# Cross attention in two halves of heads, input loaded in column halves, output root by reciprocal and square root

## The chip, the cores and the metric

The kernel runs on one core of a Trainium2 chip. The metric is the device time of one execution in microseconds; the median of three timed runs is compared. The core has TensorE (PE in the rows; PEld is its weight load), VectorE (DVE), ScalarE (ACT), GpSimd (POOL) and SyncE (SP), which run their own instruction streams and wait for one another by semaphores.

## The reference, cut to what matters

Activations are x, 256 x 1024 in fp32. Two layers of a first block (three branches: spatial gating, attention, gated linear attention) are followed by one layer of a second block: three mixers, then a cross attention, then a feed-forward and an output norm. The change touches the start of the first layer, the cross attention and the output norm.

```python
def rmsnorm(x, w):
    y = xf * lax.rsqrt(jnp.mean(xf * xf, axis=-1, keepdims=True) + EPS)
    return (y * w)

def memory_cross_attention(h, mem_n, w_q, w_kv, w_o):          # 4 heads of 256, 256 memory rows
    q = (h @ w_q).reshape(b, s, XA_HEADS, XA_HEAD_DIM)
    kk, vv = jnp.split(mem_n @ w_kv, 2, axis=-1)
    ...
    logits = jnp.einsum('bshd,bmhd->bhsm', q, kk) * XA_HEAD_DIM ** -0.5
    p = jax.nn.softmax(logits, axis=-1)
    o = jnp.einsum('bhsm,bmhd->bshd', p, vv).reshape(b, s, XA_HEADS * XA_HEAD_DIM)
    return o @ w_o

x = x + memory_cross_attention(rmsnorm(x, norm_xa_w), rmsnorm(mem, norm_mem_w), w_xq, w_xkv, w_xo)
h = rmsnorm(x, norm_ffn_w)
x = x + jnp.square(jax.nn.relu(h @ w_ff1)) @ w_ff2
return rmsnorm(x, norm_out_w)
```

## The kernel before

Everything stays in SBUF; only the weights stream. x is kept transposed (xT, 8 pieces of 128 columns by 256 rows; two pieces are one group g). A weight product is made from split operands: each operand is a high half (rounded to fp32r by ACT) and a low half (what is left, by DVE), and `split_mm` (L466 to L468) issues three products for one. Weights come in **chunks** of up to 128 x 1024 numbers: SP issues the DMA of chunk c into one of six places of `ring` (L2979), as soon as what used that place is done (`release`); ACT's `weights_hi` makes the high half into one of four places of `ring_hi` (L2343), for which the chunk four before must be used; DVE's `weights_lo` makes the low half (L1341); PE takes the chunk (`take_chunk`). A slot of weight columns is four chunks.

The order of each engine's work is written out by hand. In DVE's and ACT's programs of the second block, `lo_until(n)` and `hi_until(n)` mean: make low or high halves until n chunks of that block are made, then go on with what is written next. Semaphore waits between the engines hold the order together. `open_bank` gives out the eight PSUM banks in turn; a bank is opened when its last use has been freed by the reader (`free`). `hold` keeps the banks of a slot while it accumulates; `copied` waits until a bank has been read out.

**Start.** SP loads the two row halves of x (L2960), then the chunks. POOL issues the DMA of `positions` (L2837), sets `ones` (L2839), the identity and 16 constants (L2845). PE runs seven products of `ones` with itself into an unused bank (L630), then turns the norm's gains (L635) and x (L642), four groups, one bank each. DVE copies each group to xT (L1365); ACT splits from xT (L2326), DVE makes the low half (L1369); chunks 0 to 5 are split between the groups. Slot 0 (`p1(0)`, 416 columns) uses chunks 0 to 3, slot 1 chunks 4 to 7, slot 2 chunks 8 to 11. The squares of x (L2331) are added by DVE (L1376 to L1378), summed over the partitions by PE (L480) behind chunk 4, and `rms` turns the sum into rx (L1385), by shifts and three Newton steps. ACT scales slot 0 by rx on the way out (L2361) and then makes the squares on which the next norm hangs; that norm's root, its scaling and then the low half of chunk 10 follow on DVE.

**Cross attention.** In chunks of the second block: 56 to 59 are the first half of w_xq, 60 to 63 the second, 64 to 67 the last quarter of w_xkv (values of heads 2 and 3; the other keys and values are made earlier), 68 to 75 w_xo. PE's order: xq 0, xq 1, scores of all heads (L1281), the values, turns of the weights (L845), output products (L1294), out projection (wxo). DVE takes maxima and subtracts them (L2242, L2243), ACT takes exponentials of one row half, all heads (L2787), DVE sums and divides (L2248 to L2250), ACT copies the turned weights (L2794) and makes high halves of the outputs (L2355), DVE low halves (L1397).

**Tail.** The last product is made for row half 0 and 1, columns in halves. DVE adds the product to x (L2293), ACT sums the squares (L2823), DVE adds the two sums, scales, and takes the root by `rsqrt` (11 instructions, L1326 to L1331), ACT and DVE scale one column half each, and ACT and SP store it (L2827, L2982).

## Time and profile before

| | |
|---|---|
| timed runs | 1052.29 us median (1050.08, 1052.29, 1054.33) |
| profiled execution | 1050.27 us, span 1048.5 us |
| PE busy | 1013.1 us, 97% of the span |
| DVE busy | 750.2 us, 72% |
| ACT busy | 569.4 us, 54% |
| POOL busy | 73.4 us, 7% |
| DMA | 160.56 MB, 153 GB/s on average |
| TensorE clock granted, mean | 0.992 of 2.4 GHz |

The span is the time from the first to the last instruction; the rest of the profiled execution's time lies around it. Busy times overlap between engines. In the rows below a start and a duration are in us from the span's start; what stands in brackets is how long the engine had been idle before the row's first instruction, and what released it.

### The profile page before, as it was taken

The numbers are of one execution on the slowest core, as the hardware profiler recorded it, in microseconds if no ns is written. First come the engines' busy times: TensorE is split into PE (matmuls) and PEld (weight loads), VectorE is DVE, ScalarE is ACT, GpSimd is POOL, SyncE is SP. The second block draws the span as 40 slices with busy tenths as digits, with TensorE's granted clock in tenths as the row PEclk, the third lists the DMA queues.
The fourth block names the chain that finished last, engine by engine and source line by source line (L and its number), as shares of the span: only waits on it lengthen the run. The fifth ranks groups of instructions, "written<-read, shape, count | busy, mean of one in ns | idle before, by whom it ended". The sixth has DMA issues, their size and how long they took to land.

```text
span 1048.5 us, 21688 instructions
## 1 busy us (share of the span) xinstructions
PE 1013.1 (97%) x9123; PEld 929.9 (89%) x9123; DVE 750.2 (72%) x1200; ACT 569.4 (54%) x833; POOL 73.4 (7%) x177
## 2 busy tenths in 40 slices
PE   7999999999999999999999999889999999999996
PEld 6878999999977999999998998778899799998885
DVE  6879677788877966688789868755786566555445
ACT  5775576444765667453568563134354456675332
POOL 8700000020000000011240000000000000000000
PEclk9999999999999999999999999999999999999998
DMA  9645554575665544548787340011364255665551
GB/s 320 181 135 165 140 156 110 158 252 172 197 175 143 150 136 138 142 134 239 181 216 180 107 152 24 23 35 51 121 201 141 84 183 181 176 182 193 188 190 70
DMA packets 73296, 160.56 MB, mean 153 GB/s; under 512 B 6917, under 2 KB 16320, under 8 KB 73200
## 3 DMA queue, kind: packets, MB, share of 16 engines
q1 hardware_dynamic: 70048, 150.59, 47.0%
q0 software_dynamic: 2832, 8.06, 3.9%
q8 instruction: 72, 1.18, 0.5%
q10 hardware_dynamic: 320, 0.53, 0.1%
q14 instruction: 24, 0.20, 0.1%
HBM read 158.11 MB, written 1.05 MB: 152 GB/s over the span
## 4 chain that ended last, share of the span: by engine, by line
PE 88%; DVE 6%; ACT 3%; issue 2%; DMA 1%; SPq 0%; ACTq 0%; DVEq 0%
PE psum L466 24%; PE psum L468 23%; PE psum L467 23%; PE psum L856 2%; PE psum L1008 2%; DMA ring<-in_w_in 1%; DVE ring_lo L1341 1%; PE psum L845 1%; PE psum L697 1%; PE psum L675 1%; PE psum L1294 1%; PE psum L1281 1%; DVE arena L1501 1%; PE psum L689 1%; PE psum L679 1%
## 5 line engine op out<-in xcount | busy, mean ns | idle before, releaser
L1341 DVE TENSOR_TENSOR ring_lo<-ring,ring_hi 128x1024 fp32r<-128x1024 f32 (+4 forms) x292 | 343.6, 1194 | 185.5 <-ACT ring_hi L2343 183.6
L2343 ACT ACTIVATE ring_hi<-ring 128x1024 fp32r<-128x1024 f32 (+4 forms) x292 | 298.9, 1033 | 280.7 <-PE psum L468 258.0
L466 PE MATMUL psum<-hT,ring_hi 128*128 128x256 f32 x904 | 257.5, 285 | 1.5 <-issue 1.5
L467 PE MATMUL psum<-hT,ring_hi 128*128 128x256 f32 x904 | 254.7, 282 | 0.3 <-issue 0.3
L468 PE MATMUL psum<-hT,ring_lo 128*128 128x256 f32 x904 | 254.9, 282 | 0.0
L466 PEld LDWEIGHTS psum<-hT,ring_hi 128*128 128x128 f32 x904 | 171.6, 190 | 3.9 <-issue 3.4
L467 PEld LDWEIGHTS psum<-hT,ring_hi 128*128 128x128 f32 x904 | 171.6, 190 | 0.5 <-issue 0.5
L468 PEld LDWEIGHTS psum<-hT,ring_lo 128*128 128x128 f32 x904 | 171.7, 190 | 0.0
L466 PE MATMUL psum<-ring_hi,hT 128*128 128x512 f32 (+4 forms) x416 | 156.5, 376 | 4.4 <-DVE ring_lo L1341 4.4
L468 PE MATMUL psum<-ring_hi,hT 128*128 128x512 f32 (+4 forms) x416 | 152.7, 367 | 0.0
L467 PE MATMUL psum<-ring_lo,hT 128*128 128x512 f32 (+4 forms) x416 | 152.3, 366 | 0.0
L466 PE MATMUL psum<-arena_r,ring_hi 128*128 128x256 f32 x384 | 108.9, 284 | 2.2 <-DVE flag L1400 1.5
L467 PE MATMUL psum<-arena_r,ring_hi 128*128 128x256 f32 x384 | 108.2, 282 | 0.0
L468 PE MATMUL psum<-arena_r,ring_lo 128*128 128x256 f32 x384 | 108.2, 282 | 0.0
L466 PEld LDWEIGHTS psum<-ring_hi,hT 128*128 128x128 f32 x416 | 78.6, 189 | 19.0 <-issue 5.8
L468 PEld LDWEIGHTS psum<-ring_hi,hT 128*128 128x128 f32 x416 | 78.5, 189 | 11.2
L467 PEld LDWEIGHTS psum<-ring_lo,hT 128*128 128x128 f32 x416 | 78.6, 189 | 10.8 <-issue 0.5
L466 PEld LDWEIGHTS psum<-arena_r,ring_hi 128*128 128x128 f32 x384 | 72.8, 190 | 3.1 <-DVE flag L1400 1.9
L468 PEld LDWEIGHTS psum<-arena_r,ring_lo 128*128 128x128 f32 x384 | 72.9, 190 | 0.0
L467 PEld LDWEIGHTS psum<-arena_r,ring_hi 128*128 128x128 f32 x384 | 72.8, 190 | 0.0
L2361 ACT ACTIVATE arena<-psum 128x384 f32<-128x384 f32 (+4 forms) x103 | 52.4, 582 | 29.6 <-PE psum L1008 12.5
L466 PE MATMUL psum<-ring_hi,arena_r 128*128 128x512 f32 x128 | 50.3, 393 | 0.4 <-DVE ring_lo L1341 0.4
(453 smaller groups left out, 1345.6 us busy)
## 6 DMA issues: line engine op xcount, KB each, us to landing
ring<-in_w_in SPq DMA_DIRECT2D x104, 512.0 KB, 3.6
ring<-in_w_ff SPq DMA_DIRECT2D x64, 512.0 KB, 3.6
ring<-in_w_branch SPq DMA_DIRECT2D x24, 512.0 KB, 3.7
ring<-in_w_out SPq DMA_DIRECT2D x24, 512.0 KB, 3.5
ring<-in_w_in SPq DMA_DIRECT2D x24, 384.0 KB, 3.3
ring<-in_w_xkv SPq DMA_DIRECT2D x16, 512.0 KB, 3.7
ring<-in_w_in SPq DMA_DIRECT2D x8, 528.0 KB, 3.7
ring<-in_w_xq SPq DMA_DIRECT2D x8, 512.0 KB, 3.7
```

The costliest lines, as they stand in the source:

```text
L466: mm(b, lhs[0], rhs[0], start=start, stop=False, **how)
L467: mm(b, lhs[0], rhs[1], start=False, stop=False, **how)
L468: return mm(b, lhs[1], rhs[0], start=False, stop=stop, **how)
L675: m = mm(b[:, 0:384], cT[:, k, t * P:(t + 1) * P], wuq[:, k, h * 384:(h + 1) * 384], start=(k == 0), stop=(k == 1))
L679: filled(mm(b, cT[:, 2, t * P:(t + 1) * P], wukv[:, h * BANK:(h + 1) * BANK], start=True, stop=True), ("ukv", l, t, h))
L689: m = turn_(b[0:MQK, k * P:(k + 1) * P], qk[:, t, 4 * g + k, :], ident[:, :])
L697: m = mm(b[:, h * n:(h + 1) * n], qkT[0:MQK, h0 + h, t * P:(t + 1) * P], qkT[0:MQK, MH + h0 + h, 0:n], start=True, stop=True)
L856: m = mm(banks[d][q, h * n:(h + 1) * n], lhs(d, h, q), rhs(d, h, q), start=True, stop=True)
L1008: m = mm(banks[z][CH * to:CH * to + CH, o:o + CH], rhs[0](c, odd, d, p, slice(CH * row, CH * row + CH)), rhs[1](c, odd, d, p, slice(CH * r ...
L1341: V.tensor_tensor(chunk_view(ring_lo, RAW, c), chunk_view(ring, RAW, c), plain(chunk_view(ring_hi, RING_HI, c)), ALU.subtract).then_inc(ev ...
L2343: AC(chunk_view(ring_hi, RING_HI, c), chunk_view(ring, RAW, c), ACT.Copy).then_inc(ev("whi_ready"), 1)
L2361: af(AC(dst, b, func, scale=scale), free(name))
```

## The change

- Start: x is loaded in two column halves; the second is issued behind chunk 0. POOL issues the DMA of positions behind the 16 constants. ACT runs one small Copy at once. PE's products of ones are twelve, and seven more behind the turns of the first half of x. The turns of the second half come behind chunk 0 of slot 0. ACT and DVE split x from PSUM; the copy to xT comes behind the squares, which ACT now makes from PSUM. Chunk 0 is split in halves, and PE can begin with the first. The sum of squares on PE comes behind chunk 5.
- Cross attention: heads 0 and 1 go through scores, softmax and outputs before heads 2 and 3. The values' chunks are spread over the order, and so is the start of the out projection. The chunk order in the ring follows that.
- Tail: each sum of squares is scaled and added in one instruction; the root is ACT's Sqrt of DVE's reciprocal, with one Newton step for three; an idle Sqrt stands ahead of it. At row half 1, DVE's share of the scaling is done on a product made before.

```diff
-            w_cols(A["w_xq_2"][0], BANK * i, BANK)
-        w_cols(A["w_xkv_2"][0], BANK * 3, BANK)
+        w_cols(A["w_xq_2"][0], 0, BANK)
+        w_cols(A["w_xkv_2"][0], BANK * 3, BANK, part=range(1))
+        w_cols(A["w_xq_2"][0], BANK, BANK)
+        w_cols(A["w_xkv_2"][0], BANK * 3, BANK, part=range(1, CHUNKS))
         for i in range(2):
             w_rows(A["w_xo_2"][0], 4 * P * i)
...
+                    w = take_chunk(first and c == 0)
                     n = w[0].shape[2] // parts
+                    if first and c == 0:
+                        for j in range(2):
+                            if j:
+                                pe.wait_ge(ev("xlo_ready"), x_parts[0])
+                                pe.wait_ge(ev("wlo_ready"), 1)
+                            for t in range(T):
+                                m = split_mm(banks[(*tag, t, 0)][:, 0:n], parts_of(lhs, j, slice(t * P, (t + 1) * P)),
...
+                for _ in range(n):
+                    mm(psum[:, 7, 0:P], ones[:, :], ones[:, :], start=True, stop=True)
+            warmed(12)
...
-            pe.wait_ge(ev("x_in"), 16 * T)
...
+            def input_turns(half):
+                pe.wait_ge(ev(f"x_in{half}"), 16)
+                for g in (2 * half, 2 * half + 1):
...
+            input_turns(0)
+            warmed(7)
...
-                p1(0)
+                p1(0, {} if l else {0: lambda: input_turns(1)})
...
-                p1(1, {0: squares_sum(l)})
+                p1(1, {0 if l else 1: squares_sum(l)})
...
             x_parts[:] = [KD * 3, CHUNKS]
-            for i in range(2):
...
                         for k in range(2):
                             i = 2 * (2 * g + h) + k
...
+                pe.wait_ge(ev("xp_ready"), g + 1)
...
+            def attention_out(g):
...
+                copied(pe, *[("xpT", t, g) for t in range(T)], *[("xv", g, t, 0) for t in range(T)])
...
+                    filled(m, ("xo", h))
+            gemm_T(("xq", 0), xaT)
+            next(values)
+            squares_sum(3)()
+            attention_scores(0)
+            gemm_T(("xq", 1), xaT)
+            attention_turns(0)
+            next(values)
+            attention_scores(1)
+            attention_out(0)
+            next(values)
+            run(values)
+            attention_turns(1)
+            mixed = rows_T_steps(("wxo",), x_oT, KD, lambda k: pe.wait_ge(ev("lo_made"), SPLITS1 * DEPTH + 6 + (k // 2 + 1 if k < 6 else XH)))
+            next(mixed)
+            next(mixed)
+            attention_out(1)
+            run(mixed)
...
+                b = full(dve, ("x0", g))
...
+                dst = xT[:, 2 * g:2 * g + 2, :].rearrange("p a b -> p (a b)")
+                dve.wait_ge(ev("sq_ready"), g + 1)
...
+                lo_next[0] += 1
...
                 else:
-                    residual(l, ("x0",), R_NORM, (0, 1, 1, 0, 2))
-                weights_lo(2)
+                    input_low(0)
+                    first_weights_lo()
+                    input_low(1)
+                    weights_lo(1)
+                    input_low(2)
+                    weights_lo(1)
+                    input_low(3)
+                    weights_lo(1)
+                    weights_lo(1)
+                    for g in range(4):
+                        input_kept(g)
+                    weights_lo(1)
+                if l:
+                    weights_lo(2)
...
-            lo_until(65)
+            lo_until(63)
...
+                v(V.tensor_reduce(smax[:, 2 * t:2 * t + 2], b, X, ALU.max))
+                vf(V.tensor_tensor(x_s[:, t, 2 * g:2 * g + 2, :], b, bc(smax[:, 2 * t:2 * t + 2], 2, S), ALU.subtract), free(n))
+            def attention_parts(g):
+                for t in range(T):
+                    dve.wait_ge(ev("xe_ready"), 2 * g + t + 1)
+                    v(V.tensor_reduce(ssum[:, 2 * t:2 * t + 2], x_s[:, t, 2 * g:2 * g + 2, :], X, ALU.add))
+                v(V.reciprocal(ssum[:, 0:4], ssum[:, 0:4]))
+                x4 = x_s[:, :, 2 * g:2 * g + 2, :]
+                vf(V.tensor_tensor(x4, x4, bc(ssum[:, 0:4].rearrange("p (t h) -> p t h", t=T), 3, S), ALU.mult), "xp_ready")
...
+            lo_until(66)
+            attention_parts(0)
+            lo_until(69)
             attention_maxima(0, 1)
-            attention_maxima(1, 0)
             attention_maxima(1, 1)
-            attention_parts(0)
             attention_parts(1)
-            lo_until(72)
-            for h in range(XH):
-                b = full(dve, ("xo", h)).rearrange("p (a b) -> p a b", a=2)
-                low(("xo", h), b, x_oT[:, 1, 2 * h:2 * h + 2, :], x_oT[:, 0, 2 * h:2 * h + 2, :], 1.0)
+            attention_low(0)
+            lo_until(73)
+            attention_low(1)
...
-                    vf(V.tensor_tensor(final[:, t, 0, :], xn[:, t * D:t * D + BANK], out_g[:, 0:BANK], ALU.mult))
...
-                v(V.tensor_tensor(rin[:, 0:1], ssq[:, 2 * t:2 * t + 1], ssq[:, 2 * t + 1:2 * t + 2], ALU.add))
-                v(V.tensor_scalar(rin[:, 0:1], rin[:, 0:1], 1.0 / D, EPS, ALU.mult, ALU.add))
-                rsqrt(1)
-                v(V.tensor_copy(rx[:, t:t + 1], rout[:, 0:1]), "final_rms")
...
-                    v(V.scalar_tensor_tensor(out=final[:, t, 1, :], in0=xn[:, t * D + BANK:(t + 1) * D], scalar=rx[:, t:t + 1],
-                                             in1=out_g[:, BANK:D], op0=ALU.mult, op1=ALU.mult), "out_ready")
...
+                dst = xn[:, t * D + c0:t * D + c0 + n]
+                b = full(dve, ("f2", t, c0 // BANK))[:, c0 % BANK:c0 % BANK + n]
+                v(V.scalar_tensor_tensor(out=dst, in0=b, scalar=rx_more[:, t:t + 1], in1=dst, op0=ALU.mult, op1=ALU.add), "out_sum")
+                flat = final[:, t, :, :].rearrange("p h n -> p (h n)")
+                vf(V.tensor_tensor(flat[:, c0:c0 + n], dst, out_g[:, c0:c0 + n], ALU.mult))
+            def out_square(i, before):
+                dve.wait_ge(ev("final_ssq"), i + 1)
+                if before is None:
+                    v(V.tensor_scalar(rin[:, i:i + 1], ssq[:, i:i + 1], 1.0 / D, EPS, ALU.mult, ALU.add))
                 else:
-                    vf(V.tensor_scalar(final[:, t, 0, :], final[:, t, 0, :], rx[:, t:t + 1], None, ALU.mult), "out_ready")
+                    v(V.scalar_tensor_tensor(out=rin[:, i:i + 1], in0=ssq[:, i:i + 1], scalar=1.0 / D, in1=rin[:, before:before + 1],
+                                             op0=ALU.mult, op1=ALU.add))
+            def out_root(t, i):
+                r, y, z = rin[:, i:i + 1], rout[:, t:t + 1], rtmp[:, t:t + 1]
+                v(V.reciprocal(z, r), "final_inverse")
+                dve.wait_ge(ev("final_root"), t + 1)
+                v(V.tensor_tensor(z, y, y, ALU.mult))
+                v(V.scalar_tensor_tensor(out=z, in0=z, scalar=-0.5, in1=r, op0=ALU.mult, op1=ALU.mult))
+                v(V.scalar_tensor_tensor(out=rx[:, t:t + 1], in0=z, scalar=1.5, in1=y, op0=ALU.add, op1=ALU.mult), "final_rms")
+                vf(V.tensor_scalar(final[:, t, t, :], final[:, t, t, :], rx[:, t:t + 1], None, ALU.mult), "out_ready")
+            out_piece(0, 0, BANK)
+            out_piece(0, BANK, BANK)
+            out_square(0, None)
+            out_square(1, 0)
+            out_root(0, 1)
+            out_piece(1, 0, BANK)
+            out_square(2, None)
+            out_piece(1, BANK, BANK)
+            out_square(3, 2)
+            out_root(1, 3)
...
+                    if i == 0:
+                        act.wait_ge(ev("xlo_ready"), 2 * g + 2)
+                    src = xT[:, 2 * g:2 * g + 2, :] if i else full(act, ("x0", g)).rearrange("p (a b) -> p a b", a=2)
+                    af(AC(x_sq[:, 2 * g:2 * g + 2, :], src, ACT.Square), "sq_ready")
...
+                b = full(act, ("x0", g))
+                for k in (2 * g, 2 * g + 1):
+                    af(AC(hT[:, 0, k, :], b[:, k % 2 * S:(k % 2 + 1) * S], ACT.Copy, scale=cols[:, R_NORM + k:R_NORM + k + 1]),
...
+                act.wait_ge(ev("raw_full0"), landed(0))
+                for j, name in enumerate(("whi_half", "whi_ready")):
+                    AC(chunk_view(ring_hi, RING_HI, 0)[:, j, :], chunk_view(ring, RAW, 0)[:, j, :], ACT.Copy).then_inc(ev(name), 1)
...
             act.dma_start(rows[R_NORM:R_MIX, :], A["norm_g"].rearrange("l (k p) -> (l k) p", p=P)).then_inc(ev("norm_in"), 16)
+            act.wait_ge(ev("ones_ready"), 1)
...
                 else:
-                    residual_hi(("x0",), R_NORM, 0)
+                    copied(act, "norm_cols")
+                    input_hi(0)
+                    first_weights_hi()
+                    input_hi(1)
                     weights_hi(1)
-                    residual_hi(("x0",), R_NORM, 1)
+                    input_hi(2)
                     weights_hi(1)
-                    residual_hi(("x0",), R_NORM, 2)
-                    weights_hi(1)
-                    residual_hi(("x0",), R_NORM, 3)
-                    weights_hi(1)
-                squares()
-                weights_hi(6)
+                    input_hi(3)
+                    weights_hi(2)
+                squares(l)
+                weights_hi(6 if l else 5)
                 act.wait_ge(ev("rx_ready"), l + 1)
                 p1(0)
...
+            def attention_exp(g):
...
                 act.wait_ge(ev("xs_scale"), 1)
...
+                for t in range(T):
+                    copied(act, ("xs", t, g))
+                    s1 = x_s[:, t, 2 * g:2 * g + 2, :].rearrange("p h n -> p (h n)")
+                    af(AC(s1, s1, ACT.Exp, scale=rx_more[:, t:t + 1]), "xe_ready")
+            def attention_turned(g):
...
+            def attention_high(g):
...
+            hi_until(65)
+            attention_exp(0)
+            hi_until(68)
+            copy_out(("xq", 1, 0), xq_T[:, 4:6, :], BANK, shape=2)
+            copy_out(("xq", 1, 1), xq_T[:, 6:8, :], BANK, shape=2)
+            attention_turned(0)
+            hi_until(69)
+            attention_exp(1)
+            attention_high(0)
+            hi_until(70)
+            memory_v(1)
             hi_until(72)
-            for h in range(XH):
-                high(("xo", h), x_oT[:, 0, 2 * h:2 * h + 2, :], 2)
+            attention_turned(1)
+            hi_until(73)
+            attention_high(1)
...
+            a(AC(rtmp[:, 2:3], rx[:, 0:1], ACT.Sqrt))
...
+                a(AC(at(proj_all, 2048, n), xn[:, t * D + c0:t * D + c0 + n], ACT.Square, accum_out=ssq[:, i:i + 1]), "final_ssq")
...
+                act.wait_ge(ev("final_inverse"), t + 1)
+                a(AC(rout[:, t:t + 1], rtmp[:, t:t + 1], ACT.Sqrt), "final_root")
                 act.wait_ge(ev("final_rms"), t + 1)
                 h = 1 - t
                 a(AC(final[:, t, h, :], final[:, t, h, :], ACT.Copy, scale=rx[:, t:t + 1]), "half_ready")
                 act.dma_start(out[0, t * P:(t + 1) * P, h * BANK:(h + 1) * BANK], final[:, t, h, :]).then_inc(ev("stored"), 16)
+            out_sums(0, 0, 0, BANK)
+            out_sums(1, 0, BANK, BANK)
+            out_root(0)
+            out_sums(2, 1, 0, BANK)
+            out_sums(3, 1, BANK, BANK)
+            out_root(1)
...
-            pool.dma_start(posi[:, :], A["positions"].rearrange("a (t p) -> p (a t)", p=P),
...
+                           allow_slow_non_contiguous=True).then_inc(ev("pos_in"), 16)
             def masks():
...
         @block.sync
         def _(sp_):
-            for t in range(T):
-                sp_.dma_start(xn[:, t * D:(t + 1) * D], A["x"][0, t * P:(t + 1) * P, :]).then_inc(ev("x_in"), 16)
+            def input_half(half):
+                sp_.dma_start(at(xn, 0, T, D)[:, :, half * BANK:(half + 1) * BANK],
+                              A["x"][0].rearrange("(t p) d -> p t d", p=P)[:, :, half * BANK:(half + 1) * BANK]).then_inc(ev(f"x_in{half}"), 16)
+            input_half(0)
             for c, (parts, _, _) in enumerate(chunks):
+                if c == 1:
+                    input_half(1)
```

## Rows read from the trace of the kernel before

**Rows 1.** Page, part 1: busy time, share of the span, instructions.
```profile
PE 1013.1 (97%) x9123; PEld 929.9 (89%) x9123; DVE 750.2 (72%) x1200; ACT 569.4 (54%) x833; POOL 73.4 (7%) x177
```

**Rows 2.** Page, part 4: the chain that ended last, by engine.
```profile
PE 88%; DVE 6%; ACT 3%; issue 2%; DMA 1%; SPq 0%; ACTq 0%; DVEq 0%
```

**Rows 3.** Chain of waits in order of time (start us, us, what), start.
```profile
1.73 6.61 DMA ring<-in_w_in
8.37 0.91 ACT ring_hi L2343
```

**Rows 4.** Timeline from 0 to 34 us (start us, us, engine, line, operation, tiles).
```profile
1.27 1.28 ACT L2326 ACT_TABLE_LOAD   x1 [1.27 <-PEq L3000]
1.33 0.87 POOL L2837 DMA_DIRECT2D posi<-in_positions  x1 [0.81 <-POOLq L3000]
...
2.48 3.16 PE L630 MATMUL psum<-ones 128*128 128x128 f32 x14 [2.48 <-POOL ones L2839]
...
10.47 0.42 PE L466 MATMUL psum<-ring_hi,hT 128*128 128x416 f32 x1 [2.67 <-DVE ring_lo L1341]
...
16.16 0.43 PE L466 MATMUL psum<-ring_hi,hT 128*128 128x416 f32 x1 [0.72 <-DVE ring_lo L1341]
...
20.77 0.26 PE L657 MATMUL psum<-ident,arena 107*128 107x107 f32 x1
```

**Rows 5.** DMA rate, 0 to 20 us in 40 slices of 0.5 us.
```profile
GB/s 0 0 0 8 147 377 369 377 442 390 306 137 107 223 276 369 396 403 406 402 411 401 411 406 397 401 397 410 374 221 268 395 471 373 406 381 426 418 393 424
```

**Rows 6.** Timeline of ACT, then of DVE, 17 to 60 us.
```profile
29.46 1.11 ACT L2361 ACTIVATE proj<-psum,rx 128x416 f32<-128x416 f32 x2 [0.77 <-DVE rx L1385]
...
36.15 1.22 DVE L1341 TENSOR_TENSOR ring_lo<-ring,ring_hi 128x1024 fp32r<-128x1024 f32 x1
```

**Rows 7.** Timeline of PE: the first instruction on chunk 10.
```profile
38.71 0.39 PE L466 MATMUL psum<-ring_hi,hT 128*128 128x512 f32 x1
```

**Rows 8.** PE's waits, 785 to 857 us (total us, times, longest).
```profile
PE psum L466 <- DVE flag L1400: 1.5, 1, 1.5
PE psum L1294 <- ACT arena L2794: 1.1, 1, 1.1
PE psum L1281 <- issue: 0.8, 1, 0.8
```

**Rows 9.** Timeline of PE, windows within 800 to 827 us.
```profile
804.50 1.75 PE L1281 MATMUL psum<-proj,arena 128*128 128x256 f32 x7 [0.84 <-issue]
...
811.29 0.58 PE L466 MATMUL psum<-ring_hi,hT 128*128 128x512 f32 x1
...
822.57 1.91 PE L845 MATMUL psum<-ident,arena 128*128 128x128 f32 x16
```

**Rows 10.** Timeline of DVE and ACT, softmax.
```profile
806.50 0.69 DVE L2242 TENSOR_REDUCE smax<-psum 128x2 f32<-128x512 f32 x1
...
814.66 1.23 DVE L2250 TENSOR_TENSOR arena<-arena,ssum 128x1024 f32<-128x1024 f32 x1
...
809.79 1.15 ACT L2787 ACTIVATE arena<-arena,rx_more 128x1024 f32<-128x1024 f32 x1 [4.57 <-issue]
```

**Rows 11.** Timeline of the tail.
```profile
1041.74 0.19 ACT L2823 ACTIVATION_READ_ACCUMULATOR proj<-xn 128x1 f32 x1
1041.96 0.16 DVE L2300 TENSOR_TENSOR rin<-ssq 128x1 f32<-128x1 f32 x1
...
1044.71 0.72 ACT L2826 ACTIVATE proj<-proj,rx 128x512 f32<-128x512 f32 x1 [2.78 <-DVE rx L2303]
```

**Rows 12.** Groups of ACT's instructions over the span (busy us, mean ns).
```profile
L2683 ACT ACTIVATE rtmp<-na_sum 128x1 f32<-128x1 f32 x4 | 0.8, 202 | 0.1
...
L2468 ACT ACT_TABLE_LOAD x2 | 2.6, 1283 | 0.0
```

**Rows 13.** Stretches (from:to, length, busy by engine, PEclk, DMA share, GB/s).
```profile
664.00:667.00 3.00, 1.22 (x51) 1.02 (x45) 2.78 (x6) 0.18 (x1) 0.00 (x0) 1.00 0.00 0
667.00:672.00 5.00, 4.31 (x144) 3.94 (x144) 3.88 (x14) 1.01 (x3) 0.00 (x0) 0.66 0.01 3
```

159 lines of the change are left out of this document (71 added, 88 removed).

## Prediction

> **What bounds the kernel now.** I read the page first. PE is busy 1013.1 of 1048.5 us [rows 1], and the chain that ended last is 88% PE [rows 2]. The change removes no product of PE, so it can only win where PE stands still, or where the chain leaves PE: at most the other 12%. The diff touches three such places: the start, the cross attention (about 785 to 857 us) and the tail behind the last product. I then read each from the view that shows what ends last there: chain and timeline for the start, PE's waits for the attention, the timeline for the tail. The profiled execution took 1050.27 us, its span 1048.5; the median of the three timed runs is 1052.29, their mean 1052.2 (1050.08 to 1054.33). The sum is made against 1050.27 and then carried to the timed runs.
>
> **The start.** Today the chain begins with the DMA of weight chunk 0, issued at 1.73 and landed 6.61 us later, at 8.34; ACT makes its high half at 8.37 in 0.91 [rows 3], DVE the low half, and the first product runs at 10.47; PE waits 2.67 us for that [rows 4]. Why so late a landing? The DMA rate is about 370 to 440 GB/s from 2.5 us on, then falls to 137 and 107 GB/s in two slices near 6 us and comes back only near 7.5 [rows 5], though chunks are queued. The positions DMA, 4 byte elements on POOL's queue, was issued at 1.33 [rows 4]. I take it to be the cause (the row shows the coincidence, not the cause). The change issues it behind POOL's 16 constants, and orders half of x, chunk 0, other half, chunk 1. In front of chunk 0 then lie 0.5 MB and not 1.0, which at 400 GB/s is 1.3 us less, and no dip: chunk 0 at about 6.0. So the landing stops ending last, and what is next is PE's warm-up.
>
> The positions issue also leaves POOL's path to the memset of ones: 0.87 us earlier, so the warm-up starts at about 1.6 and not 2.48 [rows 4]. It has 12 products for 7, two instructions each. The 14 of today take 3.16 us, 0.226 each; 24 at that rate end at 7.0. A two-instruction product of the attention, 256 wide, takes 0.25 per instruction at full clock (7 in 1.75, the pipeline's end included) [rows 9], so 0.11 at 128 wide; if PE rises to full clock after some 3 us as it must have today, the end is 5.7. I take 6.3. Then the gain columns and 4 transposes (0.12 each by 16 in 1.91 [rows 9]): group 0 of x is in PSUM at 7.0. ACT now splits it straight from PSUM (DVE's copy, 0.7 as other 128x512 pieces [rows 10], leaves the path): two ACT pieces, together about one 0.91 piece [rows 3], to 7.9; DVE's low halves as long, to 8.8; the low half of half a chunk, about half of 1.22 [rows 6], to 9.4. The second 7 warm-up products (14 instructions, 1.5 to 3.1 us, from 7.5) end at 9.0 at full clock, hidden, but at 10.6 at half clock, where they would themselves be the bound. First product: 9.4, against 10.47.
> From there PE needs 24 instructions per 4.61 us (16.16 to 20.77 [rows 4]), so 9.2 for the slot; today it takes 10.3, with the wait of 0.72 before 16.16 among it. The new order puts 8 transposes (1.0) inside the slot, which used to lie in idle time, and they cover the waits for the later splits: ACT and DVE alternate x pieces and chunks at 1.8 to 2.1 us per pair against 2.3 of PE's per chunk. End: 9.4 + 9.2 + 1.0 = 19.6 against 20.77, 1.2 us.
> Will it be kept? The next in line is the norm. ACT's copy of slot 0 waits for rx at 29.46, and the low half of chunk 10, behind that same chain, is done at 36.15 + 1.23 = 37.4 [rows 6]; PE takes it at 38.71 [rows 7]. So 1.3 us at most comes through unless rx is earlier too. rx hangs on chunks 6 and 7, whose landing today is late for DMA rate; they are now issued earlier (when chunk 0 is used) but the positions dip still comes, later. DVE's four copies of x to SBUF (0.7 each) now wait for ACT's squares behind the splits, and behind them is queued the low half of chunk 5, due on PE at 22.8, done at about 22. That fits by 0.7 us. The banks of x are freed by those copies, due at 20.0, done from 18.8. I take **1.2 us**, bounds -0.8 (half clock through both warm-ups: 10.6 + 10.2 = 20.8, and 0.7 for chunk 5) and +2.3 (rx moves too). The early table load is worth nothing: the load already runs at 1.27, ahead of all data [rows 4].
>
> **The cross attention.** PE waits in three places: 0.8 before the scores (for the copies of xq 1), 1.1 before the output products (for ACT's copies of the turned weights), 1.5 before the out projection (for DVE's low halves) [rows 8]. Counted from one instruction's start to the next they are 1.0, 1.1 and 1.7, together 3.8. The new order puts other products behind each: chunk 0 of xv (12 instructions at 0.23 wide pace, 2.8 us, from 48 in 822.57 - 811.29 [rows 9]) and the sum of squares after xq 0; xq 1 (11.5) over the first softmax; two chunks of the out projection (5.7) over the turned weights of half 1. I laid out the order from 791.75, where xq 0 ends: xv chunk 794.6, squares 794.9, scores 0 (half of 6.8: 3.4) 798.3, xq 1 809.8, turns 810.8, xv 813.6, scores 1 817.0, outputs 0 820.4, two xv chunks 826.0, turns 827.0, two chunks 832.7, outputs 1 836.1, rest of the projection 853.3.
> DVE and ACT against it: norm until 797.8, low chunk, two maxima and subtractions (4 x 0.69) to about 802, exponentials of half size (0.65; a whole one is 1.15 [rows 10]), low halves of two chunks, sums and one product of 1.23 [rows 10]: first weights at 807.8, needed at 809.8, 2.0 to spare. Copies of xq 1 and of the turned weights 811.7, needed at 813.6. Second softmax at 821.7, needed at 826.0. The closest is ACT's order at 827: copy of xv, high halves of chunks 70 and 71, and only then the copies of the turned weights, done 830.4; PE wants them at 832.7. The instructions are more (eight smaller pieces for four) but neither engine is full here. DVE's new waits (for exponentials) hold up low halves of chunks 66 and 68, due 3 us or more later. The sum is that all 3.8 goes and five more changes of product kind come, at less than 0.1 each: **3.4 us**, bounds 1.5 (one of the spare times misjudged by 2) and 3.9.
>
> **The tail.** From the end of ACT's last sum (1041.93) DVE runs 14 small instructions, 2.75 us (0.196 each), before ACT's scaling at 1044.71 [rows 11]. The change leaves: fused scale and add, reciprocal, ACT root, three for one Newton step. DVE: 5 x 0.196 = 1.0; ACT: 0.20 for one 128x1 activation [rows 12] and two handovers of 0.1 (1041.74 + 0.19 to 1041.96 is 0.03, rx to ACT 0.1): 1.4. Gain **1.4 us**; bounds 1.1 and 1.6 if no table is loaded on the path. Row 0's root falls away too, but was hidden by PE. The load of the root's table (1.28 [rows 12]) comes with the idle root behind the last high half, where ACT only waits for PE's last products: hidden, and 1.3 on the path if that cover were gone. What is last next: ACT's scaling (0.72), issue and landing, all as before.
> Does Square or Copy after the root load a table back? Rows say that loads (1.28 each) come at few lines only [rows 12], and between them the engine ran both kinds in more than one set: the first load is for a Copy [rows 4] and the Squares of the first norm follow without one.
> The Trainium skill, "ScalarE: Activation LUTs", section "Table sets: the hidden batching unit", speaks against the change: exp and root are in different sets, and cheap functions it names as in every set are relu, copy, identity, abs, not Square. By that page each switch is about 2.66 us with its drain; an estimate with two on the path would be -5.3 + 1.4. The trace has 1.28 for the load.
>
> **Sum.** 1.2 + 3.4 + 1.4 = 6.0 us: 1044.3 for the profiled execution, 1046.2 from the timed runs' mean. The profiled one lies 1.9 below it, so I put the forecast a little under the latter: **1045.8**. With the bounds of the terms the total is 1.8 to 7.8; the runs themselves scatter by 2 either way. 0.5% (5.3 us), about what a measurement of this kernel can tell from no change, is 1047.0: the forecast lies just beyond it.
>
> **Rivals.**
> A: the start gives nothing, since rx and the chunk landings set the pace until 38 us (for it: only 1.3 to spare there [rows 6, 7]). 4.8 us in all: 1047.2. Chance 0.15.
> B: one spare time in the attention is misjudged, most likely at 809.8 (2.0) or 832.7 (2.3), and a wait of 2 comes back; 4.0: 1048.0. Chance 0.09.
> C: Square is not in the root's set. Then ACT loads before the last sums and before the root, 1.28 each; the first of them is hidden when it comes early, the second is on the path, the first partly: tail +0.1 to -1.2 (1.4 less 1.28 or 2.56), total 4.0: 1048.2. This is the page's rule as a mechanism here. Chance 0.06, as the rows show Square under two sets.
> D, slower: the granted clock. It is 1.00 on average from 664 to 667, where PE was busy 1.22 of 3.0 us, and 0.66 on average from 667 to 672 [rows 13], right behind. At half clock (0.50, 1.2 GHz) for 2 x 0.34 of 5 us, 3.4 us, this costs 1.7. The changed start shifts everything behind it, and more such stretches can be caught. It decides from the fourth further one (6.8 against 6.0); with six, 10.2 - 6.0 = 4.2 slower, 1056. Against it: the attention had clock 1 throughout, and the gaps that the change leaves there are smaller. Chance 0.05.
> E: rx and landings move too and a half-clock stretch is lost: 8.5, 1043.3. Chance 0.05.
> Forecast: 0.60. The range that leaves out no more than 0.2: the terms' bounds and the scatter, **1041 to 1050.5**. Faster by over 0.5%: 0.45 of the 0.60, 0.05 of A and 0.05 of E, 0.02 of B and C, so 0.57; slower by over 0.5% 0.03 (part of D); the rest, 0.40, within.
>
> **What would show it.** First product at 9 to 10 us, not 10.5, the DMA dip behind chunk 0's landing, slot 0 over by 19.6, and at 38 us no wait of PE for a low half; PE's waits of the attention gone from their list, with first split of the residual 3.4 us sooner relative to xq 0's end; 1.35 to 1.4 between ACT's last sum and its scaling, and one table load more in the whole trace. It is wrong if PE's start is bound by the warm-up at half clock, if a wait appears at the first x banks or chunk 5, or if the root comes with a load beside it.

## The result, and the profile after

The changed kernel takes 1044.58 us (median of eight runs; 1043.2 to 1049.3) against 1050.35 for the one before (eight runs, 1048.51 to 1054.33); the ratio is 0.9942 with a 95% interval of 0.9925 to 0.9959, or 6.1 us (4.3 to 7.9). The forecast was 1045.8, and 6.0 less by the sum of the terms. Ratios use fast runs alone, which leaves out of all the runs one of the kernel before, at 3225 us. The profiled execution took 1044.02 us, its span 1042.3 (before: 1050.27 and 1048.5), so 6.25 less.

The page's busy times and the chain by engine, answering to [rows 1, 2]:

```profile
PE 1016.2 (97%) x9147; PEld 933.6 (90%) x9147; DVE 747.5 (72%) x1188; ACT 571.0 (55%) x841; POOL 71.9 (7%) x177
...
PE 86%; DVE 6%; ACT 3%; issue 3%; DMA 2%; ACTq 0%; POOL 0%; DVEq 0%; POOLq 0%
```

24 instructions of PE more are the warm-up's. What the page can't tell is where the 6.2 us come from. For that I set the start of every PE instruction of one trace against the same one of the other; the table under the experiments has these differences for all kernels. For this one: 0.9 us ahead at 20 us, 0.6 from 40 us, 0.85 behind from 245 us, 0.55 ahead again at 780 us, 4.6 from 858 us, and 6.2 at the end.

**Start.** The timeline of all engines from 0 to 31 us, after (start us, us, engine, line, operation), against [rows 4, 6, 7], and the DMA rate of the first 20 us in slices of 0.5 us, against [rows 5]:

```profile
1.08 5.00 PE L648 MATMUL psum<-ones 128*128 128x128 f32 x24 [1.08 <-POOL ones L2987]
...
6.17 1.09 PE L664 MATMUL psum<-ident,xn 128*128 128x128 f32 x8
...
6.92 0.84 ACT L2452 ACTIVATE hT<-psum,cols 128x256 fp32r<-128x256 f32 x2 [4.12 <-PE psum L664]
...
7.10 1.73 PE L648 MATMUL psum<-ones 128*128 128x128 f32 x14
7.65 0.99 ACT L2460 ACTIVATE ring_hi<-ring 128x416 fp32r<-128x416 f32 x2
...
9.40 0.43 PE L470 MATMUL psum<-ring_hi,hT 128*128 128x416 f32 x1 [0.58 <-DVE ring_lo L1430]
...
19.89 0.26 PE L682 MATMUL psum<-ident,arena 107*128 107x107 f32 x1
...
25.13 1.06 ACT L2446 ACTIVATE ring_hi<-ring 128x1024 fp32r<-128x1024 f32 x1 [0.72 <-DMA ring<-in_w_in]
...
30.08 1.11 ACT L2478 ACTIVATE proj<-psum,rx 128x416 f32<-128x416 f32 x2 [1.27 <-DVE rx L1445]
```
```profile
GB/s 0 0 0 37 70 107 226 367 389 363 395 403 413 406 390 409 393 388 393 394 400 397 385 406 395 380 406 363 270 156 172 205 254 270 369 422 381 418 424 406
```

The dip to 137 and 107 GB/s near 6 us [rows 5] is gone, and the first product runs at 9.40 for 10.47. (The later dip, to 156 GB/s near 15 us, isn't that of the positions: they had landed at 10.26.) At the end of slot 0 it is 19.89 for 20.77. Then part of it goes: the copy that waits for rx comes at 30.08, not at 29.46 [rows 6], and at 38.02 PE starts on chunk 10 some 0.2 us late.

**Cross attention.** One stretch of PE, 780 to 860 us (length, busy by engine, PEclk, DMA share, GB/s), of the kernel before and then of the changed one:

```profile
780.00:860.00 80.00, 76.55 (x543) 72.04 (x543) 50.81 (x77) 39.22 (x54) 0.00 (x0) 1.00 0.43 137
```
```profile
780.00:860.00 80.00, 80.00 (x578) 76.17 (x577) 53.26 (x82) 43.26 (x61) 0.00 (x0) 1.00 0.47 153
```

PE stood still for 3.45 us of this stretch, the three waits of [rows 8], and now not at all. From before it to behind it the lead grows from 0.55 to 4.62.

**Tail.** Its timeline after, ACT and DVE, against [rows 11]:

```profile
1037.10 0.19 ACT L2961 ACTIVATION_READ_ACCUMULATOR proj<-xn 128x1 f32 x1
1037.32 0.16 DVE L2386 SCALAR_TENSOR_TENSOR rin<-ssq,rin 128x1 f32<-128x1 f32 x1
1037.51 0.16 DVE L2392 RECIPROCAL rtmp<-rin 128x1 f32<-128x1 f32 x1
1037.77 0.20 ACT L2966 ACTIVATE rout<-rtmp 128x1 f32<-128x1 f32 x1 [0.48 <-DVE rtmp L2392]
...
1038.71 0.72 ACT L2969 ACTIVATE proj<-proj,rx 128x512 f32<-128x512 f32 x1 [0.74 <-DVE rx L2396]
```

From the end of the last sum (1037.29) to the scaling are 1.42 us, for 2.78. No table load stands between. The one further load of the whole trace is at 1025.0, while PE is still at work on the last products, so it is hidden.

**Near 240 us** the trace has a wait that the one before has not. PE's waits from 200 to 260 us, after (before: none), and ACT's from 200 to 230 us, of before and of after (total us, times, longest):

```profile
PE psum L470 <- DVE hT L1747: 1.0, 1, 1.0
```
```profile
ACT ring_hi L2343 <- DMA ring<-in_w_branch: 4.1, 2, 2.6
```
```profile
ACT ring_hi L2446 <- DMA ring<-in_w_branch: 5.9, 4, 3.8
```

In both kernels POOL issues the second layer's vectors here (2.3 MB, from 210 us on), beside SP's branch weights. After, these weights land later (the chunk issued near 213 us takes 11.1 us to land, for 8.8), and PE is 1.4 us behind for it.

### The profile page after: what moved, and what is told of

The parts are those of the page before. It is cut to its first block, busy times and chain, and to the rows that moved or that the text cites. A ratio compares the mean times of both kernels' runs of the same rounds, so it can differ in the third digit from the quotient of the medians.

```text
span 1042.3 us, 21750 instructions
## 1 busy us (share of the span) xinstructions
PE 1016.2 (97%) x9147; PEld 933.6 (90%) x9147; DVE 747.5 (72%) x1188; ACT 571.0 (55%) x841; POOL 71.9 (7%) x177
## 4 chain that ended last, share of the span: by engine, by line
PE 86%; DVE 6%; ACT 3%; issue 3%; DMA 2%; ACTq 0%; POOL 0%; DVEq 0%; POOLq 0%
PE psum L470 23%; PE psum L472 23%; PE psum L471 22%; PE psum L881 2%; PE psum L1033 1%; PE psum L870 1%; DVE ring_lo L1387 1%; DMA ring<-in_w_branch 1%; PE psum L722 1%; PE psum L700 1%; DVE arena L1573 1%; PE psum L1307 1%; PE psum L714 1%; PE psum L1324 1%; PE psum L704 1%
## 5 line engine op out<-in xcount | busy, mean ns | idle before, releaser
L2446 ACT ACTIVATE ring_hi<-ring 128x1024 fp32r<-128x1024 f32 (+4 forms) x291 | 297.7, 1034 | 267.9 <-PE psum L472 241.9
L472 PEld LDWEIGHTS psum<-ring_hi,hT 128*128 128x128 f32 x416 | 78.1, 188 | 11.1
L2478 ACT ACTIVATE arena<-psum 128x384 f32<-128x384 f32 (+4 forms) x103 | 52.8, 584 | 28.0 <-PE psum L1033 11.8
```

What stands on the lines that cost most here:

```text
L472: return mm(b, lhs[1], rhs[0], start=False, stop=stop, **how)
L2446: AC(chunk_view(ring_hi, RING_HI, c), chunk_view(ring, RAW, c), ACT.Copy).then_inc(ev("whi_ready"), 1)
L2478: af(AC(dst, b, func, scale=scale), free(name))
```

## The experiments

For each kernel its timed ratio to the kernel before, and where its profiled execution gains against that of before. The gains are differences of PE's start times, in us, worked out from the two traces: at 40 us, what is added around 240 us, in the middle (260 to 780), across the attention (780 to 860), and in the tail (the span's gain less that at the last products). A span is that of one execution: those of only_tail and late_proj are the slowest of their kernel's timed runs, that of warm_short the fastest.

```
kernel           ratio, interval          at 40   at 240   middle  attention  tail   span
after            0.9942 0.9925-0.9959      0.6    -1.4      1.4      4.1      1.6    1042.3
only_start       0.9974 0.9961-0.9988      1.1    -0.1      1.3      0.0      0.0    1046.2
only_attn        0.9948 0.9931-0.9964     -0.3     0.0      0.9      4.1      0.0    1043.9
only_tail        1.0016 1.0001-1.0031     -2.8    -2.7     -1.4      0.0      1.6    1053.9
before_again     (one execution)          -0.7     0.0     -1.5      0.0     -0.1    1050.8
warm_short       0.9956 0.9935-0.9977      0.6    -1.4      1.8      4.1      1.5    1042.0
tail_warm        1.0006 0.9991-1.0022     -0.5    -1.1      1.0      0.0      1.5    1047.6
pos_moved        0.9988 0.9965-1.0011     -0.6     0.0      0.6      0.0     -0.1    1048.5
late_proj        0.9983 0.9958-1.0009      0.3    -3.1     -2.0     -0.5      1.6    1052.2
table_back       0.9965 0.9943-0.9986      0.3    -3.0      1.6      4.1      0.3    1045.3
sqrt_only        1.0015 0.9992-1.0039     -1.0    -1.1     -1.3      0.0     -0.1    1052.0
vectors_later    0.9956 0.9940-0.9972      1.1     0.0      2.1      4.1      1.6    1044.1
vectors1_later   0.9921 0.9899-0.9944      0.9     0.0      1.0      4.1      1.6    1041.0
```

(vectors_later loses another 4.4 between 40 and 200 us.)

### The three parts alone, and the kernel before once more

only_start has the diff's edits of the start alone (the orders of x and positions, the warm-ups, the splits from PSUM, chunk 0 in halves), only_attn those of the attention and its chunk order, only_tail those of the tail. before_again is the kernel before, unchanged.

> The kernel before with the start of the change alone. My theory: the first weight product at 9.4 us (10.47 before), slot 0 over 0.9 us earlier, 0.6 us of it left behind 40 us because the norm's rx is not earlier, and no more than 0.6 us on the whole time beside the scatter of the half-clock stretches. Rival: the start is worth what it gains at slot 0 or more (1 us and above), and what was lost behind 38 us in the changed kernel was chance: then PE is 0.9 us or more ahead from 45 us on.

> The kernel before with the cross attention of the change alone. My theory: PE's waits of 0.8, 1.1 and 1.5 us are gone, and the stretch from the end of xq 0 to the end of the out projection is 4.1 us shorter, nothing else: 4 us on the whole time. Rival: part of the 4.1 us in the changed kernel came from its other position in time; then this run shows 3 us or less in that stretch, or a wait that the changed kernel doesn't have.

> The kernel before with the tail of the change alone. My theory: 1.4 us between ACT's last sum and its scaling for 2.75 to 2.8, so 1.4 us on the whole time. Rival: the rest of what the changed kernel gained behind the last product (1.6 us in all) comes from the tail too, with an earlier second store; then 1.6. A table load on the path would make it 0.1 or a loss.

> The kernel before, one more look. Theory: what differs between 40 and 785 us in the traces (half-clock stretches near 579 and 640 us, issue gaps near 710 us, the branch weights' landing at 222 us) varies from execution to execution of one kernel by 1 to 3 us, and the stretches from 785 to 857 us and behind the last product don't, by more than 0.1. Rival: the middle comes out the same to 0.2 us as in the first trace of this kernel, and then its differences belong to the change.

only_start: 2.7 us in the timed runs (1.3 to 4.1), the first product 1.4 and the end of slot 0 1.2 sooner, and 1.1 kept behind 40 us; another 1.3 comes in the middle, all of it at 710 us (under rivals D and E below). only_attn: 5.5 us in the timed runs (3.8 to 7.3), 4.07 in its place, as in the whole. only_tail: slower by 1.7 us (0.1 to 3.3), though 1.42 us stand between the last sum and the scaling there too. Its loss is elsewhere. Its chain at the start (start us, us, what), to set against [rows 3], and stretches of its start (columns as above):

```profile
1.73 8.02 DMA ring<-in_w_in
```
```profile
8.00:10.00 2.00, 0.53 (x5) 0.29 (x3) 1.43 (x3) 1.00 (x3) 1.64 (x4) 1.00 1.00 373
10.00:12.00 2.00, 0.13 (x1) 0.16 (x1) 1.30 (x2) 2.00 (x4) 2.00 (x4) 0.66 1.06 409
12.00:17.00 5.00, 5.00 (x15) 4.77 (x16) 4.93 (x10) 4.13 (x9) 4.29 (x13) 0.50 1.08 339
```

The start is that of the kernel before, instruction for instruction, and yet chunk 0 lands 1.4 us later (8.02 for 6.61). PE stands still for 3.3 us and then runs at a granted clock of 0.50, the lower level (1.2 GHz), to 17.5 us. So the old start has executions that lose 2.8 us: 1.4 by the late landing (first product at 11.87, for 10.47), 1.4 by the clock behind it. before_again puts a size to the chance in one trace: 0.7 at the start (chunk 0 lands at 8.99) and 1.5 in the middle, for nothing; its attention and its tail agree with those of before within 0.1. The columns of attention and tail can be read to 0.1 us. The sums in those of start and middle can't be read to 1 us, unless one looks where in them the time goes.

### The start: warm-up and positions

warm_short is the changed kernel with the old warm-up:

```diff
-            warmed(12)
+            warmed(7)
...
             input_turns(0)
-            warmed(7)
```

tail_warm is only_tail with seven warm-up products between x's turns and the first layer:

```diff
                 filled(m, ("x0", g))
+            for _ in range(7):
+                mm(psum[:, 7, 0:P], ones[:, :], ones[:, :], start=True, stop=True)
```

pos_moved is the kernel before with the positions' DMA behind the constants:

```diff
-            pool.dma_start(posi[:, :], A["positions"]...)
             g(G.memset(ones[:, :], 1.0), "ones_ready")
...
                 g(G.memset(freq[:, i:i + 1], ...
+            pool.dma_start(posi[:, :], A["positions"]...)
```

> The changed kernel with the warm-up of before: seven products and none behind the turns. Theory A (the added products buy a steady clock): the first weight product comes at about the same time or 0.5 us sooner, but PE idles before it and a half-clock stretch appears in the first 20 us in some or all executions, costing 1.5 to 3.5 us on the median. Rival B: the longer warm-up is itself what ends last at 6 us (24 instructions until 6.1), and shorter is 0.5 to 0.8 us faster.

> The tail alone, and seven more products of ones behind PE's turns of x, where PE idled from 8 to 11.8 us in the run of the tail alone. Theory: the tail alone was slower than its 1.4 us gain allows because the clock fell to half from 10.6 to 17.4 us behind that idle time (4.0 us of idle and 6.8 us at half clock in its trace); the products keep PE busy there, the clock stays at full, and the whole time falls from 1053.8 to below the kernel before, by some 3 to 4 us. Rival: the half clock is chance and not tied to the idle time, or the tail itself costs: then the time stays near 1053 and a half-clock stretch stands in the first 20 us again.

> The kernel before with only the DMA of the positions moved behind POOL's constants. Theory 1, this DMA makes the dip of the DMA rate near 6 us: the slices at 137 and 107 GB/s rise to 350 or more (or the dip goes with it to a later time), chunk 0 lands 0.6 to 1.5 us sooner, and the first product comes 0.3 to 1.2 us sooner, bounded by the warm-up and the copies of x, which come no sooner by more than POOL's 0.87 us. Rival: the dip is from the order of x and weights on the queues; then it stays at 6 us in place and size, the landing of chunk 0 stays within 0.3 us, and so does the first product.

Stretches of warm_short, then of the changed kernel cut alike in vectors1_later (same start):

```profile
5.00:8.00 3.00, 1.06 (x8) 0.82 (x8) 1.32 (x3) 2.28 (x6) 2.48 (x9) 0.97 1.04 387
8.00:12.00 4.00, 3.64 (x12) 3.51 (x13) 2.44 (x5) 1.07 (x2) 3.69 (x6) 0.60 1.05 399
```
```profile
8.00:12.00 4.00, 3.42 (x22) 3.18 (x22) 3.30 (x7) 1.99 (x5) 3.69 (x6) 1.00 1.05 396
```

With the short warm-up PE was busy for 1.06 of the 3 us ahead, and its first products run at a mean clock of 0.60. That costs 0.28 us at 20 us and nothing behind 40 us, since there the chain of rx is what PE waits for. The timed ratio (0.9956) can't be told from that of the changed kernel (0.9942). tail_warm has clock 1.00 throughout where only_tail had 0.50, and loses 0.5 at the start for 2.8. Chunk 0 lands at 8.29 in it, for 9.75, so 1.4 of the difference are the landing's; that the rest is the warm-up's isn't shown, as PE also had less time to stand still. In the timed runs it lies 0.1% below only_tail, and the intervals overlap.

pos_moved's DMA rate, against [rows 5], and its chain at the start:

```profile
GB/s 1 0 0 82 228 352 378 393 393 320 243 346 356 373 376 386 386 354 280 280 322 388 397 401 397 432 399 414 325 366 383 377 401 418 410 405 363 337 322 303
```
```profile
1.26 4.52 DMA xn<-in_x
```

The dip near 6 us is gone by this one edit, so that DMA makes it; from 5 to 8 us the six traces with the old issue have 217 to 274 GB/s, the eight with the new one 347 to 403. Whether a shallower dip near 9 us (280) belongs to the new issue is open, as the changed kernel, with the same issue at 4.62, has none. Chunk 0 lands at 7.48, for 8.34, and ACT takes it without a wait. But the first product is at 10.61, for 10.47: now the chain goes through x, which lands at 5.78, its turns, copies and splits. In this trace PE was slow besides. Its first weight products start every 0.35 us up to 14.1 us, like those of only_tail at a granted clock of 0.50, and not every 0.19; stretches from the first product on, of pos_moved, only_tail and before:

```profile
10.60:14.10 3.50, 3.49 (x10) 3.35 (x11) 3.43 (x7) 2.63 (x6) 3.50 (x8) 1.00 1.07 401
```
```profile
11.80:15.30 3.50, 3.43 (x10) 3.31 (x11) 3.43 (x7) 2.63 (x6) 3.35 (x8) 0.50 1.10 373
```
```profile
10.40:13.90 3.50, 3.43 (x17) 3.17 (x18) 3.43 (x7) 2.64 (x6) 3.50 (x8) 1.00 1.07 405
```

Ten products for 17 in 3.5 us, though the view gives clock 1.00 for it; the trace has no record of the clock before 14.1 us (before has none before 5.3), so that 1.00 isn't a reading. The turns of x before them went at 0.21 each, for 0.11. So in this trace the earlier landing brought nothing, but it doesn't show what it is worth with PE at full pace: four turns at the old pace would have been over some 0.4 us sooner (an estimate from these two paces). To reach 9.40 the change also has x in halves and its split from PSUM.

### The attention: the out projection's early chunks

late_proj is the changed kernel, with the first two chunks of the out projection again behind the output products:

```diff
-            next(mixed)
-            next(mixed)
             attention_out(1)
             run(mixed)
```

> The changed kernel without the two chunks of the out projection ahead of the second pair of heads' output products; all products are still made, only later. By the prediction ACT's copies of the turned weights end 5.7 - 2.3 = 3.4 us behind the point where PE would now want them, so a wait of 2.5 to 3.5 us comes back before the output products, and perhaps 0.5 for low halves before the projection: 2.5 to 4 us of the attention's gain gone. Rival: the copies come with the turns, and the kernel loses under 0.5 us, which would make this part of the new order idle.

PE's waits from 785 to 860 us, and two stretches behind the wait:

```profile
PE psum L1324 <- ACT arena L2911: 2.7, 1, 2.7
```
```profile
832.00:836.00 4.00, 1.62 (x5) 1.35 (x6) 2.36 (x2) 2.28 (x4) 0.00 (x0) 0.84 0.29 115
836.00:845.00 9.00, 9.00 (x59) 8.35 (x58) 1.21 (x2) 2.03 (x3) 0.00 (x0) 0.88 0.14 43
```

The wait is within the 2.5 to 3.5 expected from the prediction's 5.7 of cover and 2.3 to spare. What I hadn't in the sum is that the clock falls behind it: 0.16 of 4 and 0.12 of 9 us, 1.7 us. Together 4.4, against 4.5 by the start times. So the gain hangs on this one move: without it the new order is 0.5 us worse across the attention than the old one.

### The tail: a table load on its path

table_back is the changed kernel with one small exponential ahead of the last sums:

```diff
+            a(AC(rtmp[:, 3:4], rx[:, 0:1], ACT.Exp))
             out_sums(3, 1, BANK, BANK)
             out_root(1)
```

> The changed kernel with one small exponential ahead of the sums of the last row block, so that the root's table is no longer in place when the last root comes. If a table load costs what its row says (1.28 us) and its start need not wait for data, it begins behind the last Square and DVE's three instructions hide up to 0.6 us of it: 0.7 to 1.3 us more between ACT's last sum and its scaling, 2.1 to 2.7 for 1.4. If the switch costs 2.66 us with a drain, as the Trainium skill, ScalarE: Activation LUTs, Table sets: the hidden batching unit has it, 2.1 to 2.7 us more. If Square belongs to the root's set, one load; if to that of the exponential alone, none earlier. The rest of the kernel stays.

```profile
1036.78 1.28 ACT L2976 ACT_TABLE_LOAD   x1
...
1038.85 0.19 ACT L2961 ACTIVATION_READ_ACCUMULATOR proj<-xn 128x1 f32 x1
...
1039.50 1.28 ACT L2966 ACT_TABLE_LOAD   x1 [0.47 <-DVE rtmp L2392]
1040.79 0.20 ACT L2966 ACTIVATE rout<-rtmp 128x1 f32<-128x1 f32 x1
...
1041.74 0.72 ACT L2969 ACTIVATE proj<-proj,rx 128x512 f32<-128x512 f32 x1 [0.74 <-DVE rx L2396]
```

From the last sum (1039.04) to the scaling are 2.70 us, 1.28 more than in the changed kernel: the load's own duration. It doesn't begin behind the last Square, as I thought it might; it begins at 1039.50, when the reciprocal is there, so nothing hides it. In ACT's program the wait for the reciprocal stands ahead of the root, and this load stands behind the wait. That is no rule. In the changed kernel the Tanh of L2537 also stands behind a wait, for DVE, and its load runs ahead of that wait:

```profile
50.41 1.28 ACT L2537 ACT_TABLE_LOAD   x1
54.20 1.92 ACT L2537 ACTIVATE arena<-arena 128x2048 f32<-128x2048 f32 x1 [2.51 <-DVE arena L1550]
```

The load of [rows 4] at 1.27 does so too; its Copy runs at 7.25. What puts a load on one side of a wait or the other isn't shown. Had the change left a function of another table ahead of the last root, this gain would have been 0.1 and not 1.4. Square runs under both tables: here those of the last sum follow an exponential, in the changed kernel they follow a root, and neither time is a table loaded for them. The Trainium skill, "ScalarE: Activation LUTs", section "What ACT_TABLE_LOAD costs", makes its figure of 2.66 us for a switch up of a load of about 1283 ns and a drain of about 1380 ns. The load agrees with every one here (1.28 us); the drain isn't seen, the root starting 0.01 us behind the load.

### The wait near 240 us

sqrt_only is the kernel before with one instruction more, whose output nobody reads:

```diff
             for _ in range(7):
                 weights_hi()
+            a(AC(rtmp[:, 30:31], ones[:, 0:1], ACT.Sqrt))
```

vectors_later and vectors1_later are the changed kernel, in which POOL waits with the layers' vectors until the low half of the layer's tenth chunk is made: the first for both layers, the second for layer 1 alone, whose edit is this:

```diff
                 if l:
                     pool.wait_ge(ev("y2_ready"), l)
+                    pool.wait_ge(ev("wlo_ready"), LAYER_CHUNKS * l + 10)
```

> The kernel before with one instruction more: ACT takes the square root of a 128x1 column behind the last high half of the weights, as in the tail of the change, and nothing reads it. Every kernel that carries the tail edit so far shows PE waiting about 1.1 to 2.7 us near 240 us for the branch weights; no kernel without it does. Theory 1, a further table in the program (wherever it stands) is what brings the wait: it appears here, the kernel loses 1 to 3 us by 260 us against the kernel before and nothing at the start and in the attention. Theory 2, it is something else in the tail edit, or chance: no loss at 240 us, difference under 0.3 us there. In the tail itself both expect nothing, since ACT loads the table while PE works: the last sum to scaling stays at 2.8 us.

> The changed kernel, with POOL's ten DMAs of layer vectors issued only when ten chunks of that layer have been split. Theory: these 2.15 MB share the DMA engines with chunks 6 to 9 at 15 to 25 us and with the branch weights at 205 to 225 us; without them rx comes earlier, PE keeps its whole 0.9 us behind 40 us, and the wait of 1.4 us near 240 us goes: 1.5 to 2 us less in all. Rival: the chunks' landing there is bound by their own issue (their place in the ring), and the vectors move nothing, or their later place collides with chunks that are then on PE's path: no gain or a loss.

> The changed kernel with only the second layer's vectors issued later (from ten chunks of that layer on); the first layer's stay, since PE waited 2.5 us for them at 57 us when they came later. Theory: the chunk of branch weights that landed 11 us after its issue near 213 us in the changed kernel did so beside these 2.15 MB; the wait near 240 us goes, PE is 1.4 us ahead of the changed kernel from there in the profile, and the median is 0.5 to 1.5 us lower. Rival: that wait comes by chance and not in most executions: no difference on the median.

PE's waits of sqrt_only from 200 to 260 us, and those of vectors_later from 50 to 60 us with the stretch behind:

```profile
PE psum L466 <- DVE hT L1675: 0.9, 1, 0.9
```
```profile
PE psum L470 <- DVE ring_lo L1387: 2.5, 1, 2.5
```
```profile
54.00:60.00 6.00, 5.17 (x15) 3.88 (x16) 5.50 (x4) 3.40 (x3) 5.67 (x6) 0.72 0.20 73
```

The vectors are what the branch weights collide with: where they go later, the wait is gone and the 1.4 us with it. vectors1_later has the shortest span of all (1041.0, 1.3 below the changed kernel) and the best ratio, 0.9921; its interval overlaps that of the changed kernel, so the timed runs alone don't show that it is better. For layer 0 the delay is a loss, by the same collision with another chunk. The vectors are issued from 31.75 us on there, and the chunk that SP issues at 34.6 us takes 11.8 us to land, for 3.4 in the changed kernel:

```profile
46.42 1.06 ACT L2446 ACTIVATE ring_hi<-ring 128x1024 fp32r<-128x1024 f32 x1 [7.45 <-DMA ring<-in_w_in]
```

ACT's and DVE's work behind it is late, a low half among it; PE waits 2.5 us for that and the clock falls to 0.72 behind the wait.

Why the change brings this wait is another matter. The table shows a clean split: of the twelve traces in which layer 1's vectors are issued at the old place (before and before_again among them), the seven with a Sqrt of ACT in the tail all lose 1.1 to 3.1 us here, and the five without it lose nothing. The landings split alike: the sixth chunk of the branch weights, issued at 212 to 217 us, takes 10.8 to 12.8 us in the seven and 8.8 to 9.7 in the five. sqrt_only shows that one such instruction at 1034 us is enough in a trace, though up to 240 us its instructions are those of the kernel before and its table loads as well; in its timed runs nothing can be told (0.9992 to 1.0039). So the order and the amount of work there can't be the cause. What differs is the program as it lies in memory, or what the chip fetches for it. The DMA records do have the packets that fetch instructions: between 200 and 240 us there are five in before and five in sqrt_only, each within 0.7 us of its counterpart once the 1.0 us by which that trace runs late is taken off. So that doesn't tell the cause either, and nothing was tried on it. It stays open.

The same split stands at the start, where layer 0's vectors are issued: with them at the old place, chunk 7 lands at 23.9 to 24.5 us in the five traces without a Sqrt in the tail and, of the eight with one (vectors1_later is the eighth), at 24.8 to 25.5 with the new start and at 26.3 to 26.5 with the old.

For the tail alone this explains the loss at 240 us, 1.1 and 2.7 in its two traces, against 1.6 gained behind the last product.

## Why the prediction was right, and where only its sum was

**The sum.** Forecast 1.2 + 3.4 + 1.4 = 6.0; measured in their places 0.57, 4.07 and 1.61, together 6.25. Two things that the sum hadn't stand between: -1.4 at 240 us and +1.4 in the middle, which cancel. So the total is right in part by luck. (The times of the rivals A to C were carried from the forecast and from the mean of the runs by turns; B and C, both at 4.0, differ by 0.2 for it, which decides nothing.)

**Start, 1.2.** The steps to the first product came as worked out: group 0 in PSUM at 6.9 (forecast 7.0), high half of x at 7.8 (7.9), first product at 9.40 (9.4), slot 0 over at 19.89 (19.6). Within them two sizes were off and cancelled. The warm-up began at 1.08, not at 1.6, since with the positions' issue went 0.5 us of waiting ahead of it; and its 24 instructions took 5.00 us, 0.21 each, since the fast pace of 0.11 came only for its last five, from 5.3 us on, and not some 3 us after its start. The moment isn't fixed: with the same instructions the pace changes at 5.3 us in before and at 6.9 in before_again. The second warm-up (1.73) was hidden. The step that failed is "will it be kept": I took rx to stay where it was, 29.46. It depends on chunks 6 and 7, and their landing moved. In the changed kernel ACT got chunk 7 at 25.13 (before: 24.56), rx came 0.6 later, the low half of chunk 10 began at 36.75 and ended at 37.96, and PE took it at 38.02, 0.69 ahead of [rows 7]. In only_start the copy came at 29.44 and 1.1 us were kept; in table_back and late_proj at 30.4, and 0.3 were. I would call this the chance of an execution, but only_start is also the one trace with the new start and no Sqrt in the tail, and the five others with it and with layer 0's vectors at the old place all have that copy later, at 29.8 to 30.4. So in these traces the loss goes with the tail's root, as at 240 us, and why is open. That is rival A's mechanism at half its strength. The positions' dip, which I expected to come later at full size, came nowhere in the changed kernel.

**Attention, 3.4.** Right in mechanism: all three waits went and none came. The term was too small. The waits counted from start to start were 3.8, and I took 0.4 off for five more changes of product kind; measured is 4.07, so those cost nothing that shows, and 0.3 more came that I can't place. The spare times held, and late_proj measured one of them: 5.7 us of cover less 2.3 to spare, forecast as 3.4 where the wait is 2.7. Rival B didn't occur.

**Tail, 1.4.** 1.42 forecast as 1.4, from 2.78; the gain at the root is 1.36. Another 0.2 came behind the scaling: from the last store's issue to the span's end it is 2.8, for 3.1. The load was hidden where I put it, and rival C fell. In a kernel of its own the tail gave nothing: its traces lose by 240 us, and that of only_tail by a late landing at the start, which no row of one trace could show me.

**Rivals D and E, and the middle.** The clock's stretches in the middle moved rather than multiplied. One at 578 us went and one at 640 us came (638 to 645 us, before and after):

```profile
638.00:645.00 7.00, 7.00 (x113) 6.79 (x112) 6.36 (x19) 3.06 (x9) 0.00 (x0) 1.00 0.01 2
```
```profile
638.00:645.00 7.00, 7.00 (x99) 6.87 (x98) 6.74 (x19) 2.73 (x7) 0.00 (x0) 0.76 0.01 4
```

The 1.4 us that the middle gave back are no scatter. Up to 710 us the gains and losses of the middle cancel to 0.1 in this trace; then 1.35 come at once, where before has a pause of PE and this trace has none. PE's waits from 700 to 716 us, of before, before_again and the changed kernel:

```profile
PE psum L856 <- issue: 1.1, 1, 1.1
PE psum L845 <- ACT proj L2361: 0.4, 1, 0.4
PE psum L1148 <- ACT rtmp L2683: 0.2, 1, 0.2
```
```profile
PE psum L856 <- issue: 1.1, 1, 1.1
PE psum L1148 <- ACT rtmp L2683: 0.2, 1, 0.2
```
```profile
PE psum L870 <- ACT proj L2478: 0.5, 1, 0.5
```

Each of the seven traces whose PE program is longer by the new warm-up products (9147 instructions, tail_warm 9137, for 9123) gains 1.35 us between 710 and 720 us; the six others with 9123, before_again and warm_short among them, have the pause (0.8 to 1.3 us) and gain -0.1 to 0.4. before_again was expected to show this pause as one that varies, and has it unchanged. The DMA records point to the fetch of instructions: in before the pause ends at 711.26, 1.3 us behind a packet of kind "instruction" (16 KB, landed at 709.99), and the pauses that end at 634, 653, 662 and 676 us do so 1.3 to 1.6 us behind such packets as well (those at 434, 757 and 804 us don't). More instructions ahead move the places at which a block ends; that this is the cause wasn't tried. So about half of what only_start gains goes with its longer PE program, and no term of the prediction had that.

E didn't occur: rx came later, and the changed kernel has three such stretches, as before. D's mechanism is real: late_proj and vectors_later each lost 1.7 us to the clock behind waits of 2.7 and 2.5. The waits of 1.1 and 1.5 us in the attention of before had no such fall behind them. Had one of the attention's spare times been misjudged by its full 2 us, the wait could have cost up to 3.7 (2 and 1.7; an estimate, as no run has a wait of 2 there), and rival B, at 2, may have been priced too low.

## What to carry over

A gain early in a kernel is kept only as far as the next thing that doesn't move with it; look for what that thing waits for, and if it is a DMA's landing, take the gain as a range. Price a wait of PE that may come back with the clock behind it: 2.7 us cost 4.4 here. Compare parts of a kernel by the start times of the same instructions in two traces, with one trace of the unchanged kernel taken again as the measure of chance. And before you call a difference chance, see at which place it comes and which of the other kernels have it there: the 1.35 us at 710 us and the loss at 240 us each return in seven of seven.
